# A bias moved from four matmuls to a copy into PSUM: GpSimd spreads it, ScalarE puts it there, VectorE clips earlier

## The reference, cut to what matters

```
def expert_block(args):
    xb, e = args                                   # 128 rows of one expert
    gu = xb @ w_gate_up[e] + b_gate_up[e]          # 1024 -> 2048
    gate = jnp.minimum(gu[:, :D_FF], SWIGLU_LIMIT)
    up = jnp.clip(gu[:, D_FF:], -SWIGLU_LIMIT, SWIGLU_LIMIT)
    glu = gate * jax.nn.sigmoid(SWIGLU_ALPHA * gate)
    return ((up + 1.0) * glu) @ w_down[e] + b_down[e]
```

## Time and profile before

| | us |
|---|---|
| median of three runs (1755.71 to 1757.04) | 1756.38 |
| the profiled execution | 1755.91 |
| its span | 1754.3 |
| one body of the loop | 35.02 |
| PE busy in that body | 35.02 |
| VectorE busy in that body | 32.91 |
| ScalarE busy in that body | 26.45 |
| GpSimd busy in that body | 7.48 |

### The profile page before, as it was taken

The page is one execution under the profiler, slowest core; times in us unless marked ns, Lnnn a source line. Parts: engine busy times, 40 slices in busy tenths (PEclk is TensorE's granted clock), DMA queues, the critical chain, the costliest instruction groups (busy, mean ns, idle before and its releaser), DMA issues.

```text
span 1754.3 us, 23536 instructions
## 1 busy us (share of the span) xinstructions
PE 1731.1 (99%) x8315; PEld 1410.9 (80%) x8316; DVE 1339.7 (76%) x1169; ACT 1120.1 (64%) x957; POOL 293.3 (17%) x228
## 2 busy tenths in 40 slices
PE   9999999999999999999999999999999999999996
PEld 7777888888887777888888888888888888888885
DVE  6323324343346898999999999999999999999998
ACT  5534334473222467777777777777777777777777
POOL 3000000000001262222222121212121212121211
PEclk9999999999999999999999999999999999999998
DMA  8322231212332599999999999999999999999995
GB/s 293 95 96 72 75 93 51 70 57 88 101 139 85 214 348 397 357 384 385 402 367 372 368 385 373 369 377 384 370 373 380 385 369 367 381 388 369 371 367 210
DMA packets 115728, 487.96 MB, mean 278 GB/s; under 512 B 18931, under 2 KB 49683, under 8 KB 66528
## 3 DMA queue, kind: packets, MB, share of 16 engines
q1 hardware_dynamic: 99576, 455.76, 67.9%
q0 software_dynamic: 16096, 31.54, 6.4%
q10 hardware_dynamic: 8, 0.01, 0.0%
HBM read 476.22 MB, written 28.36 MB: 288 GB/s over the span
## 4 chain that ended last, share of the span: by engine, by line
PE 94%; DVE 3%; ACT 2%; issue 1%; POOLq 0%; POOL 0%; DVEq 0%; ACTq 0%
PE psA L1717 22%; PE psA L1718 22%; PE psA L1719 22%; PE psX L1719 6%; PE psX L1718 6%; PE psX L1717 6%; PE psX L1724 3%; DVE wlo L1464 1%; PE psX L1911 1%; PE psX L1896 1%; PE psA L2128 1%; ACT whi L1003 1%; PE psX L1920 1%; PE psA L2008 0%; PE psX L1856 0%
## 5 line engine op out<-in xcount | busy, mean ns | idle before, releaser
L1464 DVE TENSOR_TENSOR wlo<-raw,whi 128x2048 fp32r<-128x2048 f32 x382 | 863.6, 2289 | 61.2 <-ACT whi L1003 60.2
L1003 ACT CAST whi<-raw 128x2048 fp32r<-128x2048 f32 x382 | 724.8, 1913 | 197.3 <-PE psA L1719 178.5
L1717 PE MATMUL psA<-whi,xT_hi 128*128 128x512 f32 x1036 | 408.3, 394 | 1.9 <-issue 1.9
L1719 PE MATMUL psA<-whi,xT_lo 128*128 128x512 f32 x1036 | 404.0, 390 | 0.0
L1718 PE MATMUL psA<-wlo,xT_hi 128*128 128x512 f32 x1036 | 403.9, 390 | 0.0
L1717 PEld LDWEIGHTS psA<-whi,xT_hi 128*128 128x128 f32 x1036 | 195.0, 188 | 43.1 <-issue 3.9
L1719 PEld LDWEIGHTS psA<-whi,xT_lo 128*128 128x128 f32 x1036 | 194.8, 188 | 40.7
L1718 PEld LDWEIGHTS psA<-wlo,xT_hi 128*128 128x128 f32 x1036 | 195.1, 188 | 39.6 <-issue 0.5
L1717 PE MATMUL psX<-whi,aT_hi 128*128 128x512 f32 x496 | 195.8, 395 | 0.0
L1719 PE MATMUL psX<-whi,aT_lo 128*128 128x512 f32 x496 | 193.5, 390 | 0.0
L1718 PE MATMUL psX<-wlo,aT_hi 128*128 128x512 f32 x496 | 193.3, 390 | 0.0
(11 more groups left out here) (408 smaller groups left out, 2025.2 us busy)
## 6 DMA issues: line engine op xcount, KB each, us to landing
raw<-in_w_gate_up SPq DMA_DIRECT2D x254, 1024.0 KB, 8.7
raw<-in_w_down SPq DMA_DIRECT2D x128, 1024.0 KB, 8.1
raw<-in_w_in SPq DMA_DIRECT2D x32, 1024.0 KB, 5.5
raw<-in_w_gla_proj SPq DMA_DIRECT2D x4, 1024.0 KB, 5.1
raw<-in_w_fox_proj SPq DMA_DIRECT2D x4, 1024.0 KB, 5.3
raw<-in_w_out SPq DMA_DIRECT2D x4, 1024.0 KB, 5.0
xt<-in_x SPq DMA_DIRECT2D x4, 512.0 KB, 7.3
h_dram<-xt POOLq DMA_DIRECT2D x4, 512.0 KB, 6.0
```

Source lines behind the costliest of these rows:

```text
L1003: s_.copy(xsplit(c)[0], xraw(slot)).then_inc(hi_ready, 1)
L1464: v.tensor_tensor(lo, xraw(slot), hi.bitcast(F32), ALU.subtract).then_inc(lo_ready, 1)
L1717: mm(dst, sh, mh, start=first, stop=False)
L1719: return mm(dst, sl, mh, start=False, stop=last)
```

## The change: what it does, and the diff

For experts 2 to 31 the four bias matmuls go. In their place:

- GpSimd loads the bias row of expert e (8 KB, on partitions 0, 32, 64, 96), and copies it onto all 128 partitions by four `partition_broadcast` instructions of 512 columns, into `bias_all` (`load_row`, `spread_row`). `spread_row(i + 2)` stands in body i after the gather, and ahead of the scatter. It waits for the row, for the landing of that gather, for a scatter two before, and for `seeded`.
- ScalarE copies `bias_all` into `psA` after the silu, when the second clip is done (`seed`, 128x2048). PE's gate and up matmuls then add to it (`gate_up_seeded`, no start flag), and wait for `seeded` in place of `up_ev`.
- VectorE makes its clips before low part 11 of the body, not after it, on a wait for the last gate and up tile; and the activation product comes before low part 0 of the next body, not after it.
- Expert 2's broadcasts come once, before the loop, behind `routed` and the end of body 1's gate and up product. `lnffn_g` moves to another address, since `bias_all` takes its place. Four semaphores that counted one thing each are merged; that changes no wait.

```diff
+        def load_row(e):
+            pool.wait_ge(bias_spread, 4 * (e - 2))
+            g.dma_start(bias_row[0:P:32, :], a["b_gate_up"][0][e].rearrange("(n c) -> n c", c=512)).then_inc(brow_in, 16)
+
+        def spread_row(e):
+            pool.wait_ge(brow_in, 16 * (e - 1))
+            pool.wait_ge(xg_in, 16 * e)
+            if isinstance(e, int) and e == 2:
+                pool.wait_ge(gu_done, 2)
+            else:
+                if not isinstance(e, int) or e > 3:
+                    pool.wait_ge(y_out, 16 * (e - 3))
+                pool.wait_ge(seeded, e - 2)
+            pool.sem_inc(spreads, 1)
+            for n in range(4):
+                g.partition_broadcast(bias_all[:, n, :], bias_row[32 * n:32 * n + 1, :]).then_inc(bias_spread, 1)
+            pool.wait_ge(bias_spread, 4 * (e - 1))
...
         pool.wait_ge(routed, 1)
-        pool.wait_ge(gu_done, 2)
+        g.dma_start(bias_row[0:P:32, :], a["b_gate_up"][0][2].rearrange("(n c) -> n c", c=512)).then_inc(brow_in, 16)
+        spread_row(2)
...
             if not last:
-                pool.wait_ge(gu_done, i + 1)
-                load_bgu(i + 1)
                 if not isinstance(i, int) or i < E - 2:
+                    load_row(i + 2)
                     gather(i + 3, i + 2)
             if isinstance(i, int) and 3 <= i < 3 + TT:
                 add_bias(i - 3, i)
+            if not last and (not isinstance(i, int) or i < E - 2):
+                spread_row(i + 2)
             scatter(i - 1)
...
+        def seed(e):
+            act.wait_ge(up_ev, e)
+            act.wait_ge(bias_spread, 4 * (e - 1))
+            s_.copy(psA[:], bias_all[:]).then_inc(seeded, 1)
...
             turned_hi(xt_done, i + 2, xT_hi, xT_hi_s)
             silu(i)
+            seed(i + 1)
             for c in range(XSPL):
                 step_hi(i + 1, c)
...
-            for c in range(XSPL + 5, STEPC):
+            for c in range(XSPL + 5, STEPC - 1):
                 step_lo(i, c)
             swiglu_in(i)
+            step_lo(i, STEPC - 1)
             turned_lo(xT_hi_s, i + 2, xT_hi, xT_lo, xT_lo_s)
-            step_lo(i + 1, 0)
             swiglu_out(i)
-            for c in range(1, XSPL):
+            for c in range(XSPL):
                 step_lo(i + 1, c)
...
+        def gate_up_seeded(n, c):
+            tile_ready(n)
+            hi, lo = xsplit(c)
+            for b in range(4):
+                cols = slice(b * 512, (b + 1) * 512)
+                mm(psA[:, b, :], xT_hi[:, c, :], hi[:, cols], start=False, stop=False, skip_group_check=True)
+                mm(psA[:, b, :], xT_hi[:, c, :], lo[:, cols], start=False, stop=False, skip_group_check=True)
+                ins = mm(psA[:, b, :], xT_lo[:, c, :], hi[:, cols], start=False, stop=c == KT - 1,
+                         skip_group_check=True)
+            ins.then_inc(tile_used, 1)
...
-                pe.wait_ge(up_ev, i)
+                pe.wait_ge(seeded, i - 1)
...
-            gate_up_bias(i)
+            if first:
+                gate_up_bias(i)
```

More of the change, by code:

```diff
@@ L226, in build @@
     aT_lo = at("aT_lo", 184, [P, KT, P], F32R)
+    bias_row = at("bias_row", 182, [P, 512])
+    bias_all = at("bias_all", 120, [P, 4, 512])
     acc = at("acc", 80, [P, TT, D])
@@ L310, in build @@
     act_half, dve_half = S("act_half"), S("dve_half")
-    small_done, smT_evac = S("small_done"), S("smT_evac")
-    fl_done, fl_evac = S("fl_done"), S("fl_evac")
-    gate_pre, la_ln, la_ready = S("gate_pre"), S("la_ln"), S("la_ready")
+    smT_evac = S("smT_evac")
+    fl_evac = S("fl_evac")
+    low_product, la_ln, la_ready = S("low_product"), S("la_ln"), S("la_ready")
     suf_done, kd_exp, kd_mul = S("suf_done"), S("kd_exp"), S("kd_mul")
@@ L351, in build @@
     bgu_in = S("bgu_in")
+    brow_in, bias_spread, seeded = S("brow_in"), S("bias_spread"), S("seeded")
+    spreads = S("spreads")
     acc_in = [S(f"acc_in{t}") for t in range(TT)]
@@ L413, in down_used, with gu_used @@
         return STEPC * i + 2 * GUC + DNC if i < E - 1 else NMAIN
+    def gu_used(i):
+        return STEPC * i + DNC
     def xraw(slot):
@@ L893, in hook @@
             if s == 3:
-                act.wait_ge(small_done, 1)
+                act.wait_ge(low_product, 1)
                 for r in range(TT):
@@ L899, in hook @@
             if s == 4:
[L900 removed]
+                act.wait_ge(low_product, 2)
                 s_.copy(fl[:], psX[:, :, 0:FH]).then_inc(fl_evac, 1)
             if s == 5:
[L903 removed]
+                act.wait_ge(low_product, 3)
                 log_sigmoid_tail(la[:], psX[:]).then_inc(la_ln, 1)
@@ L1092, in _ @@
         silu(1)
+        seed(2)
         for c in range(XSPL):
@@ L1538, in swiglu_in, with swiglu_in_over, clip @@
         def swiglu_in(i):
-            dve.wait_ge(gu_done, i + 1)
+            if isinstance(i, int) and i < 2:
+                dve.wait_ge(gu_done, i + 1)
+            else:
+                dve.wait_ge(tile_used, gu_used(i))
+            clip(i)
+        def swiglu_in_over(j):
+            dve.wait_ge(gu_done, 3 + j)
+            clip(E + j)
+        def clip(i):
             v.tensor_scalar(by_pair(gate_t), psA[:, 0:2, :].rearrange("t b (q p k) -> t (b q) k p", p=P, k=2), LIMIT,
@@ L1697, in _ @@
                     tile_lo(c % XRAW, NMAIN + STEPC * j + c, c)
-                swiglu_in(E + j)
+                swiglu_in_over(j)
                 swiglu_out(E + j)
@@ L1821, in hook @@
                              start=True, stop=True)
-                ins.then_inc(fl_done, 1)
+                ins.then_inc(low_product, 1)
             if s == 5:
@@ L2079, in overflow_counts @@
                 ins = mm(psX[0:3 * E, 1, 0:1], member3[:, t, :], ones[:, 0:1], start=t == 0, stop=t == TT - 1)
-            ins.then_inc(counts_done, 1)
+            ins.then_inc(ov_product, 1)
         def overflow_ranks():
             pe.wait_ge(flag_ready, 2)
-            mm(psX[0:3 * E, 1, 1:2], strict[0:3 * E, 0:3 * E], ovflag[:], start=True, stop=True).then_inc(pre_done, 1)
+            mm(psX[0:3 * E, 1, 1:2], strict[0:3 * E, 0:3 * E], ovflag[:], start=True, stop=True).then_inc(ov_product, 1)
         def overflow_list():
@@ L2186, in body @@
             else:
-                pe.wait_ge(up_ev, i)
+                pe.wait_ge(seeded, i - 1)
             for c in range(GUC):
-                gate_up(tile_no(i, c), c, (xT1_hi, xT1_lo) if first else (xT_hi, xT_lo), first and c == 0)
+                if first:
+                    gate_up(tile_no(i, c), c, (xT1_hi, xT1_lo), c == 0)
+                else:
+                    gate_up_seeded(tile_no(i, c), c)
                 if first:
@@ L2230, in _ @@
         split_ready(xT_hi_s, xT_lo_s, E)
-        pe.wait_ge(up_ev, E - 1)
+        pe.wait_ge(seeded, E - 2)
         for c in range(GUC):
-            gate_up(tile_no(E - 1, c), c, (xT_hi, xT_lo))
+            gate_up_seeded(tile_no(E - 1, c), c)
             if c == 2:
```

26 lines of the change are left out of this document (11 added, 15 removed).

## The result

The changed kernel takes 1790.43 us (median; 1787.81 to 1797.9), the kernel before, run beside it on the same chip, 1756.17 us. The ratio is 1.0202, 95% interval 1.0189 to 1.0216: slower by 34 us. The forecast had the sign and a range that holds the time, but said +10 us. The profiled execution of the changed kernel took 1788.8 us with a span of 1787.1 us, 32.8 us more than the span before.

A forecast was written before the change was run, and what follows sets the result against it. PE was taken to bound the kernel, busy for the whole 35.02 us body, with VectorE next. From 1755.91 us, bodies -1 and start +11 gave 1766 us; forecast's own range 1758 to 1780, full range 1745 to 1795.

The forecast's parts named there:

- PE's saving: PE's body without the bias matmuls: 0.46 us less, 34.56 us; -13.8 us over 30 experts, bounds -12.9 and -15.6.
- ScalarE's copy: Bias copy from SBUF into PSUM after the silu: 1.9 us, bounds 1.8 and twice it, cost 0.
- VectorE's order: VectorE's clips and product moved earlier: waits of 0.42 and 0.66 us go, no time saved, more lead.
- The price of a broadcast: Each of four broadcasts per body: 0.65 us on GpSimd, 0.5 us lost by VectorE, 2.0 us a body.
- The wait alone is thus absorbed: In the bodies, VectorE's copies wait 2 to 3 us for the later scatter, yet tile 9 is ready before PE wants it.
- the stepping of the queues to 35.0 us: Following queues into the next body, low part 4 comes about 1 us late: body 34.6 to 35.7 us, likeliest 35.0.
- the sum of +11: Start of the loop, expert 2's row, broadcasts and first scatter: +11 us, bounds +3 and +14.
- PE standing for 6.6 us: Before body 2, PE waits for expert 2's row, broadcasts, copy and first parts: 6.6 us, taken as 7, bounds 3 and 8.
- "+4" from the first scatter: At the start, body 2's late gather makes the first scatter land near 707, holding its down tiles 4 us (0 to 5).
- That the broadcasts don't hold VectorE: Rival for the loop: body is PE's 34.56 us, start 3 to 9, total 1745 to 1752 us; 27 in 100.
- VectorE as the outright bound: Rival for the loop: broadcasts of 0.9 us and more, body 35.7 us, start +13, total 1789 us; 18 in 100.
- the first rival: The rival that broadcasts don't hold VectorE: bodies of 34.56 us, 1745 to 1752 us, about 1748; 27 in 100.

The follow-up runs named there:

- once: Changed kernel with expert 2's four broadcasts only, later experts reusing its bias (wrong results, for timing alone): 1760.03 us, ratio 1.0022.
- order_only: Kernel before with only VectorE's new order (clips one low part earlier, activation product ahead of the next tile's low part): 1755.38 us, ratio 0.9993.
- spread_first: Changed kernel with each body's four broadcasts moved ahead of the gather in GpSimd's queue: 1792.4 us, ratio 1.0208.
- best_apart: best with the down bias's four scatters in bodies 3, 5, 7 and 9 instead of 3 to 6: 1745.32 us, ratio 0.9947.
- end_iota: warm_mid plus a tiny iota after the last broadcast, ahead of body E - 2: 1772.87 us, ratio 1.0093.
- warm_mid: Changed kernel plus a one-column broadcast near 565 us, after the last iota before the expert lists: 1778.16 us, ratio 1.0133.
- warm: Changed kernel plus a one-column broadcast near 50 us, where GpSimd has nothing to do: 1790.51 us, ratio 1.0188.
- warm_end: warm plus a small affine_select after the last broadcast: 1788.91 us, ratio 1.0199.
- expert2: Changed kernel, but expert 2 gets its bias by matmuls as before and broadcasts begin with expert 3: 1776.78 us, ratio 1.0104.
- best: spread_first, expert2, warm_mid and end_iota edits together, with the down bias's scatter also ahead of the broadcasts in bodies 3 to 6: 1756.19 us, ratio 1.0004.

## Why the prediction was right or wrong, point by point

**PE's saving** was right in its mechanism and a little short: 35.02 - 34.46 = 0.56 us a body, forecast 0.46, bounds 0.43 to 0.52. With no broadcasts the loop is 15.7 us shorter than before, where the term said 13.8. The 0.52 us between matmul and transposes show most of it. Nearly all of the rest lies in the eight transposes behind them: the next matmul starts 0.85 us after the first of them before (1153.77 to 1154.62), and 0.79 in `once` (1167.91 to 1168.70).

**ScalarE's copy** cost 1.87 us and held nobody, as said. **VectorE's order** saves nothing by itself, as said (`order_only`).

**The price of a broadcast** was right for GpSimd and too high for VectorE. Four standing alone take 2.80 us, 0.70 each (forecast 0.65). What VectorE loses was 2.0 us a body in the forecast, 1.40 in the four low parts and 1.17 in its whole body (32.82 to 33.99), so 0.29 to 0.35 each where the term said 0.5. The Trainium skill's rule (SBUF — State Buffer, Who interferes with whom), that VectorE's instruction with two SBUF inputs and a reading GpSimd instruction shut each other out, is borne out: four broadcasts that take 2.80 us alone take 9.18 among low parts. That VectorE loses the full 2.80 us of a body is not borne out: it loses 1.17.

**The step that failed in the bodies** is "The wait alone is thus absorbed", and the stepping of the queues to 35.0 us behind it. The place was right: scatter behind the broadcasts (1172.44, forecast 1174.5), VectorE waiting for it ahead of its small copies, 19 times. But I gave the wait one size for every body and let a lead absorb it. VectorE, at 33.99 us of 34.46, has 0.5 us of lead in a body and no more; where VectorE waits, it takes from the scatter's issue to VectorE's copy 10.1 us (778.17 to 788.25) to 14.1 (1100.29 to 1114.43); and bodies with the down bias's scatter, which my step left out, have a chain of two landings of their own. The mean of the bodies behind the first is 35.43 us, forecast 35.0 in bounds of 34.6 to 35.7; over 29 of them that is 12.5 us. `once` shows that the broadcasts bring all of it, and `spread_first` from its eighth body on, and `best_apart` throughout, that it is what stands behind them in the queue, and not their price: in `spread_first` they still cost VectorE 0.9 us (33.70 against 32.82), and PE nothing. Where the 28.4 us between `once` and the changed kernel lie can be read from PE's starts: the same 4806 of its instructions stand in both loops, in the same order. 32 of them, each the first matmul of a tile and nearly all behind a low part of VectorE, start later by 24.35 us together; the matmuls next behind such a wait lose 1.6 us, 0.08 each; the lower clock behind the longest wait (0.66 in 905 to 910 us) costs 1.6. That is 27.55 us; the rest lies in differences under 0.06 us. The profile's idle time of PE says 18.2 us only, since it begins at a matmul's recorded end, 0.39 us after its start, where the next one could have started after 0.23.

**The step that failed in the start** is the sum of +11. Its first part, PE standing for 6.6 us, is right to 0.3 us once the pauses are gone (`end_iota`). Its second part, "+4" from the first scatter, didn't come: the first body took 37.88 us against 37.95. (Its upper bound was mis-added too: 8 + 5 = 13, not 14.) What it lacked, from the differences of the first `y_t`:
- GpSimd's pause before the first broadcasts: 694.96 - 689.76 = 5.2 us (`warm_mid`). It was kept out of the sum and named beside it, since no row of the kernel before had it. The Trainium skill states it (GPSIMD Engine Reference, Instruction dispatch): about 6 us of loading at the first call of a freshly loaded routine. The traces now agree in size: 5.5 us from the pair to the first broadcast here, and 5.98 us of idle time before the one-column broadcast of `warm`; in `warm_end` and `expert2` it was 8.1 and 8.6.
- The pause at the program's start: 689.76 - 682.77 = 7.0 us (`end_iota`). 3.6 of them stand already at the first list transfer (645.83 against 642.28), from PE's wait for `ident`. By that shift two list transfers took 5.2 us each, and expert 2's row is issued 9.4 us later (674.64 against 665.22), of which the row's quicker landing takes 2.4 back. Nothing in the trace of before could show this: it is paid by the next execution.
- The mechanism itself gives 682.77 - 674.43 = 8.3 us: ScalarE starts its four high parts of body 2 at 675.57, where it was 667.22, and `y_t` follows them at once. PE's loss is of the same size: it starts that body 6.45 us later and runs at its lower clock for a while (below: 4 x 0.50 + 4 x 0.17 = 2.7 us), 9.1 us together, less the 0.56 that it saves in the body. The forecast counted the standing alone, and no clock.

Together 5.2 + 7.0 + 8.3 = 20.5 us. The first `y_t` comes at 694.6 to 696.6 us in all seven traces that have both pauses, so the sum is firm to 2 us. Its parts are less so: `warm_end` comes to 694.96 with short list transfers and a longer pause before the broadcasts.

**A reading that was too strong.** The prediction says that ScalarE waits only for PE. Rows 6 show it waiting 2.58 us for VectorE's first clip as well, once a body. Nothing in the sum hung on it, since VectorE's new order is there to shorten that wait (1.19 us after).

**The rivals.** That the broadcasts don't hold VectorE (27 in 100) had two conditions. The first came: a loss under 0.35 us per broadcast (0.29 in the body). The second, the scatter landing no more than 1 us late, did not (up to 5.13), and it is the second that cost the time. VectorE as the outright bound (18 in 100) is out, though the time fell where I had put it: a body of 35.7 us and a start of +13 would have given 1789 by another cause. That is a warning about reading a cause off a total. In `best_apart`, where the scatter lands in time, the bodies (34.46 us against 34.56) and the time (1745.32 us against 1745 to 1752) are near those of the first rival.

The bodies' irregularity is the likely reason why executions of one kernel differ: `best` spread over 13 us, where the kernel before, run beside it, stays within 2.

## What to carry to other kernels

A wait can be absorbed only by a lead that the waiting engine still has once the change has made it busier. Work out that lead first, and follow each queue through every kind of body, the few with an extra scatter included, to the next landing.
An engine that does a new kind of operation may pay to change over to it, back again, and once more in the next execution; put the first use where the engine waits anyway, and let the program end as it begins, with the way back paid where nobody waits.
When a change moves work to an idle engine and loses, look at what stands behind the work in that engine's queue before giving up the move: here one step in that order was worth 32 us (1792.4 against 1760.82), and with the order right and the start repaired the version is 0.5% faster than the kernel before.

## What the runs showed of the hardware

- When GpSimd changes to broadcasts, it stands from a pair of MODIFY_POOL_CONFIG in its queue to the first broadcast: 5.5 to 5.8 us in most traces, 8.1 in `warm_end` and 8.6 in `expert2`. The way back is longer: 11.0 us in the changed kernel from the pair to the first select, 12.0 in `end_iota` to the iota. The pair can also stand there without a pause (the kernel before, at 2.0). No pause comes between a broadcast and an `affine_select` late in the program (1697.20), but one comes again after iotas have run in between.
- What an execution leaves loaded, the next one of the same kernel seems to find: 11.26 us of idle time at the start of the changed kernel, 0.24 before, 0.50 with an iota near the end.
- An indirect transfer that reads its indices while VectorE runs low parts end to end took 5.23 us to issue where others took 0.98 to 2.34: it ended 0.9 us after the second of two low parts (650.76 + 5.23 = 655.99 and 650.66 + 4.48 = 655.14). With the list transfers 3.2 us earlier (`end_iota`) or 2.3 us later (`warm_end`), the same two, the fourth and the seventh of eight, took 0.98 and 1.90 to 2.21.
- After standing 6.37 us, PE had a granted clock of 0.50, the 1.2 GHz level, through 680 to 684 us, and 0.83 in the next 4 us; after 16.08 us, in the changed kernel, 0.50 through 692 to 695 and 0.78 to 700. The windows of `end_iota`:

```profile
680.00:684.00 4.00, 4.00 (x10) 3.13 (x11) 4.00 (x2) 4.00 (x4) 3.73 (x2) 0.50 0.76 262
684.00:688.00 4.00, 4.00 (x16) 3.24 (x15) 4.00 (x3) 2.69 (x2) 4.00 (x3) 0.83 1.01 420
```
